# Gate arithmetic of the even layer placed ahead of the copies of the tail's last columns

## The reference, cut to what matters

```python
y = h @ P['w_in_even'][e]
q, k, v, o, ig, fg, cq, ckv, kpe = split_cols(y, EVEN_SPLIT)   # 512,512,512,512,8,8,384,256,32
logi = (ig.astype(f32).reshape(B, T, 2, ML_HEADS) + P['ml_i_bias'][e]).transpose(2, 0, 3, 1)
logf = jax.nn.log_sigmoid(fg.astype(f32).reshape(B, T, 2, ML_HEADS) + P['ml_f_bias'][e]).transpose(2, 0, 3, 1)
...
def step(carry, xs):                      # mlstm_scan, one chunk
    b = jnp.cumsum(lf, axis=-1)
    dmat = jnp.where(tril, b[..., :, None] - b[..., None, :] + li[..., None, :], -jnp.inf)
    inter = b + m[..., None]
    mq = jnp.maximum(inter, jnp.max(dmat, axis=-1))
    s = jnp.einsum('bhtd,bhsd->bhts', qc, kc) * jnp.exp(dmat - mq[..., None])
```

## Time and profile before

| | us |
|---|---|
| median of 3 runs | 1463.62 |
| lowest and highest of them | 1461.95 and 1466.84 |
| the profiled execution | 1467.7 |
| span of its trace, first to last instruction | 1465.3 |
| PE busy | 1300.8 (89% of the span) |
| DVE busy | 508.0 (35%) |
| ACT busy | 357.6 (24%) |

### The profile page before, as it was taken

The page is one execution under the profiler, slowest core; times in us unless marked ns, Lnnn a source line. Parts: engine busy times, 40 slices in busy tenths (PEclk is TensorE's granted clock), DMA queues, the critical chain, the costliest instruction groups (busy, mean ns, idle before and its releaser), DMA issues.

```text
span 1465.3 us, 16887 instructions
## 1 busy us (share of the span) xinstructions
PE 1300.8 (89%) x6386; PEld 796.3 (54%) x6386; DVE 508.0 (35%) x1061; ACT 357.6 (24%) x755; POOL 112.3 (8%) x136
## 2 busy tenths in 40 slices
PE   6999788989997998788899998989889999978893
PEld 3554675456795333333456555879788843323332
DVE  3010474322225111001364952767782421110014
ACT  2100313433212111111134422433352211111111
POOL 2400010000000111110000001000000011111100
PEclk9999888999998999999998999999999899998997
DMA  9951666356528999999533210010035579999971
GB/s 366 326 199 62 225 139 230 115 194 249 185 91 326 372 387 418 418 418 411 214 98 115 93 51 0 1 30 2 1 116 215 203 291 401 417 418 418 418 295 56
DMA packets 80725, 329.10 MB, mean 225 GB/s; under 512 B 18383, under 2 KB 19577, under 8 KB 55936
## 3 DMA queue, kind: packets, MB, share of 16 engines
q1 hardware_dynamic: 66224, 300.54, 52.8%
q0 software_dynamic: 14416, 27.41, 5.6%
HBM read 320.04 MB, written 29.53 MB: 239 GB/s over the span
## 4 chain that ended last, share of the span: by engine, by line
PE 65%; DMA 15%; DVE 11%; issue 5%; ACT 1%; SPq 0%; POOL 0%; DVEq 0%; ACTq 0%; POOLq 0%
PE psum L929 20%; PE psum L1274 12%; PE psum L1023 8%; DMA ring<-in_moe_w_up 5%; PE psum L1300 5%; DMA arena<-in_moe_w_up 4%; PE psum L955 3%; DMA wide<-in_moe_w_up 3%; PE psum L1018 2%; DMA ring<-in_ada_w 2%; DVE arena L2416 2%; DVE wide L2376 1%; PE psum L898 1%; PE psum L1257 1%; PE psum L962 1%
## 5 line engine op out<-in xcount | busy, mean ns | idle before, releaser
L929 PE MATMUL psum<-wide,ring 128*128 128x384 f32 x704 | 240.5, 502 | 4.3 <-ACT wide L1601 1.9
L929 PEld LDWEIGHTS psum<-wide,ring 128*128 128x128 f32 x704 | 165.7, 239 | 71.0 <-issue 9.9
L1274 PE MATMUL psum<-arena 128*64 128x512 f32 x480 | 149.2, 615 | 18.7 <-DMA ring<-in_moe_w_up 13.4
L1274 PE MATMUL psum<-ring,arena 128*64 128x512 f32 x384 | 138.0, 638 | 10.5 <-DMA ring<-in_moe_w_up 5.7
L929 PE MATMUL psum<-ring,wide 128*128 128x512 f32 (+2 forms) x336 | 118.2, 514 | 0.0
L2287 DVE TENSOR_TENSOR arena<-arena,psum 128x256 f32<-128x256 f32 x34 | 14.3, 422 | 287.2 <-ACT arena L1749 287.2
L1274 PEld LDWEIGHTS psum<-arena 128*64 128x64 f32 x480 | 46.2, 142 | 95.7 <-issue 95.6
L1274 PE MATMUL psum<-wide,arena 128*64 128x512 f32 x224 | 88.1, 610 | 5.8 <-DMA arena<-in_moe_w_up 5.8
L1023 PE MATMUL psum<-arena 128*128 128x128 f32 x608 | 87.4, 296 | 6.4 <-DVE arena L2021 2.6
L929 PEld LDWEIGHTS psum<-ring,wide 128*128 128x128 f32 x336 | 60.4, 199 | 57.2 <-issue 56.4
L1749 ACT ACTIVATE arena<-psum 128x256 f32<-128x256 f32 x34 | 13.1, 384 | 321.0 <-PE psum L1274 321.0
(11 more groups left out here) (512 smaller groups left out, 1741.1 us busy)
## 6 DMA issues: line engine op xcount, KB each, us to landing
ring<-in_ada_w SPq DMA_DIRECT2D x23, 2048.0 KB, 13.1
arena<-in_moe_w_gate SPq DMA_DIRECT2D x28, 1024.0 KB, 14.0
arena<-in_moe_w_up SPq DMA_DIRECT2D x28, 1024.0 KB, 18.7
arena<-in_moe_w_down SPq DMA_DIRECT2D x28, 1024.0 KB, 22.8
ring<-in_moe_w_gate SPq DMA_DIRECT2D x24, 1024.0 KB, 12.9
ring<-in_moe_w_up SPq DMA_DIRECT2D x24, 1024.0 KB, 18.7
ring<-in_moe_w_down SPq DMA_DIRECT2D x24, 1024.0 KB, 20.9
ring<-in_w_in_odd SPq DMA_DIRECT2D x7, 2048.0 KB, 9.1
```

What stands on the lines that cost most here:

```text
L929: ins = mm(out, lhs(k), rhs(k), start=(k == 0), stop=(k == n - 1))
L1274: ins = mm(psum[half, 2 + s, :].rearrange("p (w f) -> p w f", w=2), hg[s][:, k, half], buffers[UNITS[q][h] % BUFFERS][0][:, :, k, :], star ...
```

## The change

Only DVE's program is written in another order. The wait for the small parameters, the four additions of the biases, |x| and min(x, 0) stand right behind the three copies of `ta`. The copies of `tb` follow; behind the first of them stands the wait for `logarithms` and the subtraction. The copy of `cols` and of its eight columns come after the third copy of `tb`. No instruction is added or left out, and the lists of PE, ACT and SP are the same.

```diff
             for c in range(TILES):
                 dve.wait_ge(*computed("ta", c))
                 take(v.tensor_copy(tail[:, c, 0:512], bank("ta", c)), "ta", c)
-            for c in range(TILES):
-                dve.wait_ge(*computed("tb", c))
-                take(v.tensor_copy(tail[:, c, 512:TAIL], bank("tb", c)[:, 0:TAIL - 512]), "tb", c)
             dve.wait_ge(S("small_in"), SMALL)
-            dve.wait_ge(*computed("cols"))
-            take(v.tensor_copy(colsT[:], bank("cols")[:, 0:P]), "cols")
-            done(v.tensor_copy(mln[:, 1].rearrange("p d h -> p (d h)"), colsT[:, 120:128]), "n_start")
-
             for d in range(2):
                 o_(tt(li[:, d], tail[:, :, 4 * d:4 * d + 4], bc(bias_e[:, 4 * d:4 * d + 4], 1, [P, TILES, 4]), ALU.add))
                 o_(tt(lf[:, d], tail[:, :, 8 + 4 * d:12 + 4 * d], bc(bias_e[:, 8 + 4 * d:12 + 4 * d], 1, [P, TILES, 4]), ALU.add))
             done(stt(tf, lf, -1.0, lf, ALU.mult, ALU.max), "log_inputs")
             o_(ts(lf, lf, 0.0, None, ALU.min))
-            dve.wait_ge(S("logarithms"), 1)
-            done(tt(lf, lf, tf, ALU.subtract), "log_decay")
+            for c in range(TILES):
+                dve.wait_ge(*computed("tb", c))
+                take(v.tensor_copy(tail[:, c, 512:TAIL], bank("tb", c)[:, 0:TAIL - 512]), "tb", c)
+                if c == 0:
+                    dve.wait_ge(S("logarithms"), 1)
+                    done(tt(lf, lf, tf, ALU.subtract), "log_decay")
+            dve.wait_ge(*computed("cols"))
+            take(v.tensor_copy(colsT[:], bank("cols")[:, 0:P]), "cols")
+            done(v.tensor_copy(mln[:, 1].rearrange("p d h -> p (d h)"), colsT[:, 120:128]), "n_start")
+
             dve.wait_ge(*computed("cum", 0))
```

## The result

The changed kernel takes 1456.49 us (median of 20 runs, 1447.79 to 1466.15), the kernel before 1465.24 (20 runs, 1461.49 to 1473.18). The ratio is 0.9935, 95% interval 0.9914 to 0.9956: 9.5 us faster by the ratio, 8.75 by the medians. In a second group of runs the ratio was 0.9932 (0.9903 to 0.9961). The forecast was 1455.2 and 8.4 us; it was taken off a median of 3 runs of the kernel before, 1463.62, which lies 1.6 us under the median of the 20.

What follows compares the result with a forecast made beforehand. PE bounds 65% of the chain, and its 5.37 us wait for the log decay also lowers the clock. 8.52 at `MR` less 0.1 for ACT gives 8.4 us off 1463.62: 1455.2 us, range 1451.5 to 1459.5.

Steps and rivals of the forecast that it cites:

- The gates moved forward: DVE's bias additions start at 149.16 and the log decay ends at 153.57; PE's 5.37 us wait goes, 1.6 us slack.
- The added wait costs nothing: DVE stands at `logarithms` from about 150.8 to 153.4, delaying the second `tb` copy; costed at zero.
- From the sums to the spread: Sums after PE's transpose take 0.85 us at full clock; DVE's copy and the spread `R` come 6.05 us earlier.
- The clock behind it: With less PE idle time, `R` and `mod_rows` run at full clock; `MR` starts at 162.65, gain 8.52 us.
- What is late next: ACT's exponentials start about 0.4 us behind `MR`; cost between 0 and 1.3 us, 0.1 taken off.
- The gain stands to the end: Later weight slices and experts' weights are issued behind PE or DVE results, so the 8.4 us gain lasts.
- the late ACT: Rival: DVE's and ACT's small steps take 2.4 us more, PE waits 0.8, gain 7.6, time 1456.0; chance 0.04.
- the gain given back: Rival: a later transfer issued at a time that doesn't move makes PE wait; time 1463.6; chance 0.06.
- The falling clock: Rival: clock falls anyway during `R` and `mod_rows`, costing up to 2.6 us; gain 5.8, time 1457.8; chance 0.26.

Runs made afterwards that it cites:

- the first with five fillers: Kernel before, with five 512-column identity matmuls on PE ahead of the wait for the log decay, first execution: ratio 0.9984 (0.9953 to 1.0016).

## Why the prediction was right, point by point

*The gates moved forward*: |x| starts 0.82 us behind the first addition, the subtraction 154.34 − 151.18 = 3.16 us after ACT's table load (3.15). Right. PE's wait of 5.37 us went, and the slack of 1.6 us was confirmed at 1.55 by making ACT later.

*The added wait costs nothing*: right. The second `tb` ends late and nobody waits for it.

*From the sums to the spread*: 6.05 us forecast, 6.05 measured. The term for which the trace before had no row, the sums at full clock, was right at 0.85 us: with DVE free, in the experiment with `cols` behind `rr`, it is 0.85. In the changed kernel the copy comes 1.07 us after the sums' start, because it stands behind DVE's copies of `cols`, which end at 156.98. So DVE was the bound, as forecast, and by 0.2 us instead of almost nothing, since the sums start 0.16 us inside the transpose. The same experiment shows what DVE held back: 0.2 by the copies and 0.3 by the two initialisations, 0.54 in all.

*The clock behind it*: 8.52 forecast at `MR`, 8.53 measured, `R` and `mod_rows` at full clock as taken. That it fits to 0.01 is a little luck: I had PE at `MR` 0.1 us ahead of `neg_m`, but from start to start `R` took 1.98 and not 1.87, and PE came just when `neg_m` was there.

*What is late next*: this term was mis-sized. I named the right mechanism (ACT's exponentials fall behind `MR`) and took 0.1 us; it is 0.30, as the early table load shows by giving exactly this back. One cause is a slip in my working: by my own rows the exponentials start 170.25 − 165.13 = 5.12 us after the reduction, so at 158.16 + 5.12 = 163.28, which is 0.63 behind `MR` and not 0.4. The trace has 164.21 − 163.57 = 0.64. The weights were no wait, as said.

*The gain stands to the end*: right within what can be measured. The two profiled executions differ by 5.1 us in span instead of 8.2 − 0.9 = 7.3. The 2.2 us between the two are less than what two executions of one program differ by (spans of 1465.3 and 1469.0 before, 1460.2 and 1456.7 after). One place where the clock was low in one trace and not in the other, before and then after:

```profile
276.43 7.09 PE L1112 MATMUL psum<-arena 128*64 128x512 f32 x32
```

```profile
270.14 9.75 PE L1112 MATMUL psum<-arena 128*64 128x512 f32 x32
```

In the second trace of either kernel it is the other way round, 9.92 us before and 7.09 after, so this isn't the change's doing. Up to the start of this row, counted from the transpose, the gain still stands: 121.25 − 114.03 = 7.2 us in the first pair and 123.09 − 113.19 = 9.9 in the second.

*The rivals*: the late ACT and the gain given back didn't happen. The falling clock didn't happen in the changed kernel's two traces, but the experiments show how near it is. With two short waits around the sums (1.1 and 0.9 us, or 0.28 and 0.93) the clock fell in four of five traces, the exception being the first with five fillers, and it fell in the one with ACT late (1.51 and 1.24). So `R` was slow in five of six, and the fall itself stood in the second wait (four) or in the first 0.1 us of `R` (one). With one wait (1.14 or 0.59 us) it stayed up in all six. That the second wait is the cause is argued from this count; the total of idle time is higher too where there are two, 2.0 to 2.8 us against at most 1.14, and only one trace comes close to it, with a fall at 1.21 us in all. My price of up to 2.6 us for a fall was somewhat low: where both `R` and `mod_rows` were slow (3.71 and 4.93 us from start to start, against 1.98 and 3.76) it is 2.9. How often it falls in the timed runs of the changed kernel stays open, since they have no trace.

## What to carry to other kernels

When the critical engine waits for a chain of small operations on others, look at where the chain's data is complete, not at where the chain is written: here 2.3% of the tail's columns were ready 7 us ahead of their use, and the copies between them served someone who wasn't in a hurry. Cost the clock with such a wait, by taking the durations behind it from rows at full clock, and then ask what every other engine does once the critical one is earlier; the 0.3 us that were lost here went to an activation table loaded on demand. Where a run's mean granted clock is at hand, compare kernels with it in view, since most of the scatter goes with it.

## What the runs showed of the hardware that I had not expected

Fillers don't reliably hold the clock. Ten matmul instructions of 4.46 us in place of idle time kept it in one trace and not in the next of the same program (`R` 2.05 and 3.78 us). Three others further on removed one fall of 6.8 us, and the next fall lasted 6.8 us instead of 3.4. Two waits of 0.3 to 1.5 us around a few narrow matmuls were followed by a fall in five of six traces; one wait of 0.6 or 1.1 us at this place was followed by none in six. The Trainium skill (TensorE: Matmul & The Clock Gate, A second HAM failure mode: psum-queue depth-cycling) describes a clock that swings because PE stops briefly and often between groups of matmuls; these five falls behind short stops agree as far as they go. And 0.01 of the mean granted clock, which is 2% of the span or 29 us at half clock, goes with 10.7 us of time in this kernel, more than the whole change is worth.
